# Dot products of the first retrieval step moved ahead, V units and an exponential reordered, in a two-layer hybrid decoder trunk

## The reference

```
def peer_ffn(x, w_q, sub_keys, u_tab, v_tab):
    q = (xf @ w_q).reshape(t, PEER_HEADS, 2, PEER_DKEY // 2)
    scores = einsum('thpd,hpnd->thpn', q, sub_keys)
    s_top, i_top = lax.top_k(scores, PEER_TOPK)              # 16 of 128, twice per head
    cand = s_top[:, :, 0, :, None] + s_top[:, :, 1, None, :]
    best, pos = lax.top_k(cand, PEER_TOPK)                   # 16 of 256 per head
    expert_idx = take_along_axis(cand_idx, pos)
    gates = softmax(best)
    hid = gelu(einsum('td,thkd->thk', x, u_tab[expert_idx]))
    out = einsum('thk,thkd->td', gates * hid, v_tab[expert_idx])
h = h + mixed @ w_out[l]
h = h + peer_ffn(rms_norm(h, ffn_norm[l]), ...)
```

## Time and profile before

| | |
|---|---|
| median of 3 runs | 3611.53 us (3593.48 to 3629.34) |
| the profiled execution's own time | 3593.12 us |
| its span, first to last instruction | 3591.0 us |
| busy share: PE, DVE, ACT, POOL | 58%, 62%, 23%, 56% |
| mean granted TensorE clock | 0.747 of full |
| mean DMA rate | 347 GB/s |

### The profile page before, as it was taken

The page is one execution under the profiler, slowest core; times in us unless marked ns, Lnnn a source line. Parts: engine busy times, 40 slices in busy tenths (PEclk is TensorE's granted clock), DMA queues, the critical chain, the costliest instruction groups (busy, mean ns, idle before and its releaser), DMA issues.

```text
span 3591.0 us, 29548 instructions
## 1 busy us (share of the span) xinstructions
PE 2080.1 (58%) x8998; PEld 971.4 (27%) x8998; DVE 2232.8 (62%) x5005; ACT 826.0 (23%) x2504; POOL 2002.1 (56%) x2085
## 2 busy tenths in 40 slices
PE   8862675866744565485753546586674457532334
PEld 4531431433313221243311323143331233200001
DVE  4479668575597576755458656756557755657240
ACT  3312313033231302122132121312312222210211
POOL 1035546565476656535556555635646756666665
PEclk9886787987867777797776768788786668755657
DMA  8498899998999999989998879998989989999998
GB/s 278 145 341 314 291 383 351 373 397 322 358 348 361 344 393 368 388 311 345 365 381 332 320 293 410 376 347 337 340 344 358 364 320 361 408 359 384 377 369 336
DMA packets 346892, 1247.17 MB, mean 347 GB/s; under 512 B 40578, under 2 KB 40648, under 8 KB 345456
## 3 DMA queue, kind: packets, MB, share of 16 engines
q0 software_dynamic: 295744, 1075.38, 79.2%
q1 hardware_dynamic: 48368, 158.69, 11.9%
q10 hardware_dynamic: 2624, 11.21, 0.8%
HBM read 1238.94 MB, written 6.20 MB: 347 GB/s over the span
## 4 chain that ended last, share of the span: by engine, by line
issue 26%; PE 19%; another core or an unknown queue 19%; DVE 17%; POOL 11%; DMA 5%; ACT 3%; SPq 0%; DVEq 0%; ACTq 0%; POOLq 0%
PE work L968 11%; POOL ring L511 11%; DVE ring L1336 6%; PE work L937 3%; PE accs L951 2%; DMA wring<-in_w_out 1%; PE work L928 1%; DVE proj L1348 1%; DMA ring<-in_peer_u,idxU 1%; DVE proj L1344 1%; ACT arena L547 1%; DMA wring<-in_peer_wq 1%; DMA ring<-in_peer_v,idxR 1%; DVE arena L1384 1%
## 5 line engine op out<-in xcount | busy, mean ns | idle before, releaser
L511 POOL DMA_INDIRECT ring<-in_peer_u,idxU x1024 | 990.5, 967 | 846.4 <-issue 278.8
L1336 DVE CUSTOM_DVE_ANT_0 ring<-ring,n2U 128x1024 f32<-128x1024 f32 x1024 | 1207.4, 1219 | 326.2 <-DMA ring<-in_peer_u,idxU 229.9
L511 POOL DMA_INDIRECT ring<-in_peer_v,idxR x1024 | 995.4, 972 | 711.2 <-issue 277.4
L951 PE MATMUL accs<-ring,wv 128*32 128x512 f32 x4096 | 728.5, 843 | 714.3 <-DMA ring<-in_peer_v,idxR 526.0
L968 PE MATMUL work<-wring,nT 128*128 128x449 f32 (+1 forms) x1040 | 510.6, 626 | 212.4 <-DMA wring<-in_w_in 60.0
L951 PEld LDWEIGHTS accs<-ring,wv 128*32 128x32 f32 x4096 | 150.3, 137 | 1204.2 <-issue 1097.6
L968 PEld LDWEIGHTS work<-wring,nT 128*128 128x128 f32 x1040 | 211.1, 209 | 475.1 <-issue 317.3
L575 ACT ACTIVATE wv<-stack,coefR 128x32 f32<-128x32 f32 x1024 | 235.9, 309 | 356.2 <-remote 259.7
L547 ACT ACTIVATE arena<-work 128x512 f32<-128x512 f32 (+3 forms) x202 | 108.8, 564 | 564.5 <-remote 275.0
L968 PE MATMUL work<-wring,n2A 128*128 128x449 f32 x384 | 168.8, 563 | 1.0 <-ACT projB L547 1.0
L547 ACT ACTIVATE proj<-work 128x512 f32<-128x512 f32 (+1 forms) x88 | 48.8, 576 | 523.9 <-PE work L968 243.6
(11 more groups left out here) (315 smaller groups left out, 2167.0 us busy)
## 6 DMA issues: line engine op xcount, KB each, us to landing
wring<-in_w_in SPq DMA_DIRECT2D x140, 449.0 KB
wring<-in_peer_wq SPq DMA_DIRECT2D x64, 512.0 KB
wring<-in_w_out SPq DMA_DIRECT2D x60, 512.0 KB
ring<-in_peer_u,idxU POOLq DMA_INDIRECT x1024
ring<-in_peer_v,idxR POOLq DMA_INDIRECT x1024
held<-in_w_in SPq DMA_DIRECT2D x20, 449.0 KB, 8.4
held<-in_peer_wq SPq DMA_DIRECT2D x16, 512.0 KB, 6.6
arena<-keys_scr ACTq DMA_DIRECT2D x8, 1024.0 KB
```

Of the source, the lines that this page charges most:

```text
L511: nc.gpsimd.indirect_dma_start(ring[:, s * D:(s + 1) * D], None, table, bass.IndirectOffsetOnAxis(ap=idx, axis=0)).then_inc(row_in[s], 16)
L951: ins = nc.tensor.matmul(acc[c][quarter(r), :], wv[:, d * QUARTER:(d + 1) * QUARTER], ring[:, s * D + 512 * c:s * D + 512 * c + 512], star ...
L1336: V.tensor_tensor_reduce(out=rw, in0=rw, in1=n2U[:], scale=1.0, scalar=0.0, op0=ALU.mult, op1=ALU.add, accum_out=hid[:, kk:kk + 1]).then_i ...
```

## The change

It touches steps 0 and 1 of the order only; after step 1 both orders have done 129 U units and 22 V units, and steps 2 to 8 are the same.

```
 PLAN = {
-    0: 'sc:N r4:U r5:U r6:UU r7:U r8:UU r9:UUU r10:U r13:U r14:U r15:U r16:U r18:UU r19:U r20:U',
-    1: 'n0:UUUUUUUUU n1:UUUU pj1:UU pj2:U pj3:UUUU xT:UUUUU pj4:R pj5:UUU pj6:UUUUUUU pj7:UU cN:UU kbT:UUUUUU X0:GCU L1:UU L2:UUV L3:UV L4:UVU L5:RUUU L6:UUUUU wT:UUUU vn:VUU sn:V y:UV at1:V at3:V pv3:UUUUU op1:UUUUUU wq0:UUUUUUUUUUUUUUUUU wq1:UU wq2:UUUU wq3:UUUU sc:UUGU r2:CV r3:V r4:V r5:V r6:VV r9:V r12:V r14:V r15:NVU r18:VV r19:V r20:VR',
+    0: 'sc:N r9:U r10:UUUUUUUUUUUUUU r11:RUUUUUU r12:UUUUUU r13:UUUUUU r14:UUUUU r15:UUUUU r16:UUUUU r17:UUUUU r18:UUUUU r19:UUUUU r20:U r21:G',
+    1: 'xT:C pj5:V pj6:VUU pj7:UU conv:VU cN:UUUU kbT:VUUU X0:VU L1:UV L2:UU L3:UV L4:UV L5:UUV L6:RUV wT:UUV vn:UU sn:V y:UV at1:UV at2:UV at3:V pv3:UUUU op1:UUUUUU wq0:UUUUUUUUUUUUUUUU wq1:UUU wq2:UUU wq3:UUUU sc:G r2:C r3:V r6:V r9:V r12:V r14:V r15:NU r18:V r20:R',
...
@@ block.sync, tables()
                 sp.dma_start(par_scr[1], par1).then_inc(pro_scr, 16)
+                sp.wait_ge(pro_keyT, 4)
+                sp.dma_start(keys_scr[0], keys_out[:, 0:2048]).then_inc(pro_keys0, 16)
...
@@ block.scalar, stage_t
-                if t:
-                    keys_load()
+                if t == 0:
+                    act.wait_ge(pro_keys0, 16)
+                keys_load()
                 mix("nm")
...
                     act.wait_ge(pro_keyT, 8)
-                    for l in range(DEPTH):
-                        act.dma_start(keys_scr[l], keys_out[:, 2048 * l:2048 * l + 2048]).then_inc(pro_scr, 16)
+                    act.dma_start(keys_scr[1], keys_out[:, 2048:4096]).then_inc(pro_scr, 16)
...
                 if t == 0:
-                    act.wait_ge(pro_scr, 16 * 7)
-                    keys_load()
+                    act.wait_ge(pro_scr, 16 * 6)
...
                     for c in range(2):
                         for i in range(8):
                             mix(f"{r}{11 * c + i}")
-                        second_out(2 * c)
+                        if c:
+                            second_out(2)
                         act.wait_ge(S["gates_arg"], nth("gates_arg", k, c + 1))
                         b = best_of(k)[:, HALF * c:HALF * c + HALF]
                         nc.scalar.activation(b, b, ACT.Exp).then_inc(S["gates_exp"], 1)
+                        if c == 0:
+                            second_out(0)
                         for i in range(8, 11):
                             mix(f"{r}{11 * c + i}")
                         second_out(2 * c + 1)
```

More of the change, by code:

```diff
@@ L307, in build @@
         pro_strip, pro_gain, pro_taps, pro_rest = sem("pro_strip"), sem("pro_gain"), sem("pro_taps"), sem("pro_rest")
-        pro_gates = sem("pro_gates")
+        pro_gates, pro_keys0 = sem("pro_gates"), sem("pro_keys0")
         pro_chain, met, pro_ffn = sem("pro_chain"), sem("steps_met"), sem("pro_ffn")
```

## The result

The changed kernel takes 3638.28 us (median of 18 runs, 3618.03 to 3670.41), the kernel before 3610.9 us in 18 runs beside it (3590.4 to 3633.45). The ratio is 1.0093, 95% interval 1.0069 to 1.0116: 0.9% slower. The predicted time, 3608 us, is 30 us short and the range holds the measured one, but "no difference" was wrong. The profiled execution of the changed kernel has a span of 3656.5 us, a slow one for its runs, so its rows are read by stage and not by their end.

A forecast was written before the change was run, and what follows sets the result against it. Bound by stage: DVE in picks, a PE-ACT-DVE chain in levels, DMA nearly full in places. Terms +10 + 0 - 5 - 8 = -3 us against 3593.1 gave 3590, or 3608 us as runs' median; range 3574 to 3640 us.

The forecast's parts named there:

- Part 1: Start of the picks: writing layer 0's keys from SP's queue shortens the wait before the first scores, -1.0 us (-1.9 to 0).
- Part 2: Lower picks: shorter exponential wait; upper picks start at 233 us with 15 dots, a lead of 11.5 us including part 1.
- Rival C: Lower picks: the exponential still comes late through ACT's stalls; lead only 5 us, total 3615 us; chance 0.10.
- Part 3: Upper picks: 85.6 us with DMA full throughout; first convolution tap at 322.6 us with 64 dots, lead 7.6 us.
- a sign of being wrong: Upper picks: the prediction is wrong if the DVE waits for rows there by more than 10 us.
- Rival B: Upper picks: gathers starve weights, tile 1's product ends past 318 us; up to +25 us, 3635 us; chance 0.15.
- Part 4: Head of step 1: fewer dots hide less, DVE waits about 5 us (0 to +8); levels start at 367 us.
- Part 5: Levels to y: -6 us for fewer dots, +5 for more V units; 75 us, y ending about 10 us later.
- V term: Levels: four more V units in the chain, priced by PE time half hidden behind ACT's copy, +5 us (0 to +16).
- Part 6: Rest of step 1: 0 us (-5 to +5) from y to wq3, -5 (-9 to 0) in the picks from fewer V units.
- Part 7: Head of step 2: V units done sooner leave the ring full with 15 gathers, -8 us (-13 to 0).
- Rival A: Windows with slack DMA: earlier gathers fill them and pay in full, up to 40 us gone, 3572 us; chance 0.17.

The follow-up runs named there:

- run 2: The change's order of units with the code of the kernel before (keys written last, block copies ahead of the exponential); ratio 1.0098 to the kernel before.
- run 4: Changed kernel with two dots per place in the upper picks: 35 dots in step 0, the other 29 in n0 to pj3 of step 1; ratio 1.0049.
- run 1: Changed kernel with the order of the kernel before put back, so only the change's code stays; ratio 0.9998 to the kernel before.
- run 3: Changed kernel with step 1's V units back at the places of the kernel before, six up to y in place of thirteen; ratio 1.0015.
- the control: The changed kernel with nothing edited, run beside the repeated half-row, half-matmul and late-V-unit kernels; ratio 1.0093 to the kernel before.
- run 11: Changed kernel with V units late, at the places of the kernel before, repeated beside the unedited changed kernel; ratio 1.0034 to the kernel before.
- run 7: Changed kernel with both order moves undone: V units late and 35 dots in step 0; ratio 1.0042, in the 3194 us set.
- run 8: Run 7's kernel with the upper exponential, too, ahead of the projection's blocks on ACT; ratio 1.0035, in the 3194 us set.
- run 9: Changed kernel with half-size rows gathered for step 1's 22 V units, repeated beside the unedited changed kernel; ratio 1.0071 to the kernel before.
- runs 5 to 8: The 3194 us set, on the changed kernel: half rows 1.0076, half matmuls 1.0072, V units late with 35 dots 1.0042, that plus upper exponential first 1.0035.

## Why the prediction was wrong

**Part 1, keys: right.** -1.0 forecast; the first pick is at 169.6 us, where it was 170.7.

**Part 2, lower picks: right in sum.** The wait was to fall to 7 us and fell to 9.37; the upper picks start at 229.9 us, forecast 233, with the 15 dots. ACT's second stall shrank as argued (9.98 to 3.74 us). Rival C is out. But run 2 puts in doubt that this lead was worth its microseconds: with the wait at 24.60 us the ratio is the changed kernel's, to within 0.4%.

**Part 3, upper picks: the term of DMA at full rate was mis-sized.** 85.6 us were forecast, 100.4 came. The DVE's own work was right: 85.48 us busy. The other bound, 42.8 MB at 409 GB/s ending at 319.6 us, was too kind: from 213.4 us the windows moved 304 x 16.5 + 392 x 100.4 = 44.4 MB, 108.5 us at 409 GB/s, to 321.9 us even if never short of full; the other 8.4 us to 330.3 are the 0.83 ahead of the picks and the 392 GB/s within. I took two bounds that met as if both could be had at once; 14.9 us of DVE idle lie between. Ten waits for rows, 10.3 us in sum and the last at 302.46 us, are most of it, just over the 10 us that the prediction had named as a sign of being wrong; behind that the DVE is busy for 26.6 of 27.3 us. So the rows pace the picks first and the DVE paces them last. Run 4 gives 8.0 us back up to the first tap, and 0.5% of the whole against run 2, by moving 29 dots to where the DVE has nothing else to wait for.

**Rival B: its mechanism didn't happen.** The last matmuls of tile 1's product, in PE's timeline:

```profile
289.62 1.77 PE L972 MATMUL work<-wring,nT 128*128 128x449 f32 x4 [0.63 <-DMA wring<-in_w_in]
292.03 1.78 PE L972 MATMUL work<-wring,nT 128*128 128x449 f32 x4 [0.64 <-DMA wring<-in_w_in]
```

The product ends at 293.7 us, not past 318 as the rival needs, and not past 300 as the forecast had it, a piece every 2.41 us. The queues from 229.9 to 293.6 us, gathers and weights:

```profile
q0 software_dynamic: 4064, 14.82, 58.0%
q1 hardware_dynamic: 3481, 11.17, 44.5%
```

So the weights got 44.5 against 58.0 here, and 17.0 against 85.7 at the head of step 2. The Trainium skill ("DMA: Bandwidth & Descriptors", Queues, rings and completion order) has a DMA engine go round its queues packet by packet. The even share that I worked out from it, and had set aside for the earlier trace rows, is nearly what this stretch shows; the earlier trace rows shows a stretch in which it is not. It is the dots that paid: near the product's end their rows come one in 2.4 us, and [1.17 <-DMA] above is one of the ten waits.

**Part 4: right.** A DVE wait of 5.36 us ahead of the gates, 5 forecast.

**Part 5: the step that failed, with its V term.** For the dots moved away and the gates' wait, parts 4 and 5 have -14.6 + 5 - 6 = -15.6 us; with the V units late the stretch from first tap to state went from 123.4 to 103.1 and 103.3 us, so -20: that side was right and a little better (against the 118.4 us of run 1 it is -15). The V units were put at +5 (0 to +16). They cost 16.5 us in the set with a control (119.8 - 103.3), and 24.0 us between the changed kernel's first profile and run 3. I had taken the price from PE's 1.92 to 3.64 us; half of PE's work left out changed nothing there, and half of the gathers gave 19.4 us. The row to go by was the earlier trace rows: four gathers at 1.24 us are 5 us per unit, in an order that all engines share, not 5 us for all of them. Between X0 and state the late units have 26 gathers and the early ones 42: 16 more, 19.8 us of issuing, and the stretch is 13.8 us longer. That price fits only the slower speed; in the 3194 us set the stretch doesn't follow the count (last section).

**Part 6: wrong sign.** 0 and -5 were forecast, +6.5 and +2.9 came (+3.4 and -0.7 in the control's profile, against the same rows of before). With the V units late the first of these two stages is 56.2 and 58.2 us, as before the change, so its loss is the early units' as well; half the gathers didn't win it back (62.1 us). For the second, early or late units make no difference to be told (130.4 and 126.8, against 129.0 and 127.2 us), so the -5 didn't come; half the gathers took 12 us from it. No experiment shows why the eight units taken out of it gave nothing.

**Part 7: right.** -8 forecast, -8.4 measured; it is bought with the early units, since runs 3 and 11 lose it (93.5 and 92.8 us).

**The sum.** From -3 to +35.6 us are 38.6: 9.9 up to the first tap (332.5 for 322.6), 14.7 from there to the state update, where the forecast gains 11 and the trace loses 3.7, 14.4 in part 6, and -0.4 in part 7. By the changed kernel's second profile against run 1's, both from sets near 3560 us, the same four are 12.1, 12.4, 4.4 and 2.6. Up to the first tap the forecast is off by about as much as from there to the state update, and by the ratios of one set each, run 4 wins back 0.5% and run 11 0.6%: part 3's rate of rows is the second term that failed, beside part 5's V units. The 0.9% does lie within the 1% to which the chance of 0.82 was given, but on the other side of nothing, and the runs can tell it from nothing. Rival A fell: in the windows with room in DMA the earlier gathers were issued, DMA rose from 0.77 to 0.87, and the chain of the levels got longer (X0 to state 61.2 to 74.4 and 67.1 us).

**Left open: what ACT, PE and DVE stand for in the levels.** The timeline of the unedited changed kernel in its second set shows one such stand. The D product is issued at 382.30 us; the DVE subtracts its result at 390.82 us, though idle for 10.77 us, and PE and ACT follow it. GpSimd issues throughout.

```profile
382.30 1.16 PE L941 MATMUL work<-arena,proj 128*128 128x128 f32 x8
...
384.15 0.94 POOL L513 DMA_INDIRECT ring<-in_peer_v,idxR  x1 [0.30 <-issue]
...
390.82 0.69 DVE L1542 TENSOR_TENSOR arena<-arena,work 128x512 f32<-128x512 f32 x1 [10.77 <-remote]
391.61 2.05 PE L941 MATMUL work<-arena 128*128 128x128 f32 x8 [7.26 <-issue]
...
395.19 0.60 ACT L549 ACTIVATE arena<-work 128x512 f32<-128x512 f32 x1 [13.70 <-remote]
```

With half the gathers ACT has one wait over 6 us that begins between X0 and state, where the control has four. Full DMA is not the condition (the half rows have one of 15.6 us there, with DMA at 0.70), and half of the matmuls doesn't remove them. The Trainium skill ("Runtime: NRT & Kernel Launch", Instruction fetch mechanics) says that an engine refills its instructions by DMA and that this is mostly hidden. The trace records the packets of such refills, and they speak against them as the cause. Of the control's 63 stands of ACT over 5 us with the releaser "remote", 28 have no instruction packet in them or in the 1.5 us ahead; 35 have one, but with the packets' moments shifted round the span in steps of 37 us it is 30 on average (23 to 37), so 35 is no more than chance gives. The kernels of the 3194 us set have as many instruction packets and no such stand. A refill that leaves no packet at that moment isn't excluded, so the cause stays open; shown is only that, at the slower speed, the loss goes with the number of gathers in the stretch.

## What to carry to other kernels

Price a unit of work by everything that all engines queue for, not by its longest instruction: here a V unit looked like 2 us of TensorE, and what it cost went with its four gathers in a shared order. Where two estimates of a stretch, one by the engine and one by the transfers, come out equal, neither is the forecast; add what is lost while they alternate, or keep the stretch thinner. A wait that is long isn't yet a wait that costs: undo it alone (run 2) before moving other work for its sake. And put the unedited kernel into every set: the kernel before had medians from 3194 to 3611 us here.

## What the runs showed of the hardware that was not expected

- The kernel before took medians of 3560, 3194, 3559 and 3599 us in four sets, and what an order is worth went with it: the order with both moves undone was 0.4% slower than before at 3194 us, and nearly the same order with four units moved 0.3% faster than before, or equal, at 3599 us. At 3194 us DMA averaged 388 and 389 GB/s over the span (runs 7 and 8), for the same 1247 MB, against 341 to 352 in the other sets. No run shows what makes the speed.
- In that set X0 to state doesn't follow the count of gathers: 43.50 us with 35 of them (half rows, which took 69.40 us with 44 at the slower speed), 48.00 with 39 (half matmuls), 44.90 with 26 (run 7, V units late):

```profile
376.60:420.10 43.50, 38.61 (x300) 25.44 (x293) 29.32 (x48) 14.07 (x49) 33.03 (x35) 0.95 0.82 266
383.10:431.10 48.00, 36.45 (x248) 26.91 (x244) 29.30 (x47) 14.22 (x49) 36.41 (x39) 0.86 1.02 406
366.30:411.20 44.90, 38.59 (x256) 29.51 (x260) 29.00 (x48) 15.04 (x53) 23.57 (x26) 0.81 0.75 274
```

- ACT's stands without a named releaser go with that speed. The page's group of ACT's copies between the levels, in the kernel of run 8 first and then in the control of run 9, with the idle time in front of them:

```profile
L549 ACT ACTIVATE arena<-work 128x512 f32<-128x512 f32 (+3 forms) x202 | 107.5, 563 | 413.7 <-PE work L938 196.6
```

```profile
L549 ACT ACTIVATE arena<-work 128x512 f32<-128x512 f32 (+3 forms) x202 | 109.3, 564 | 550.9 <-remote 235.5
```

In ACT's whole timeline none of these stands is over 5 us at 3194 us (runs 5 to 8), and the control has 63.

- Bytes and gathers came apart: 22 to 23 MB less gave back 0.2%, less than the intervals can tell, when each row of 88 gathers was halved, and 1.9%, against the changed kernel of another set, when 42 of the gathers were gone.
